# The second half of a two-stage decoder step, rebuilt: one projection stage in fp32r parts and 64 unrolled attention steps

## What is computed

```python
D_MODEL, SEQ, DEC_BATCH, DEC_SEQ, PAST_LEN, PAGE_SIZE = 1024, 1024, 8, 4, 512, 128
H_B, DQK_B, DV_B = 8, 64, 128                  # 8 heads, two maps of 64 each, values of 128

def shared_kv(x, c, g_kv, ada_w_kv, ada_b_kv, w_k, w_v, g_k):
    h, _ = ada_mod(x, c, g_kv, ada_w_kv, ada_b_kv, 2)        # rms_norm, scale, shift
    k = rms_norm((h @ w_k).reshape(b_, t_, H_B, 2, DQK_B), g_k)
    v = (h @ w_v).reshape(b_, t_, H_B, DV_B)
    return k, v                                              # both are outputs too

def diff_weights(s, lam):                                    # s: scores - slope * distance, causal
    p = jax.nn.softmax(s, axis=-1)
    return p[:, :, 0] - lam * p[:, :, 1]

def diff_block(x, c, attend, lam, lam_init, norm_g, ada_w, ada_b, w_in, g_q, g_sub, w_out):
    h, (gate,) = ada_mod(x, c, norm_g, ada_w, ada_b, 3)
    q, z = jnp.split(h @ w_in, [QB], axis=-1)
    q = rms_norm(q.reshape(b_, t_, H_B, 2, DQK_B), g_q)
    o = attend(q, lam)                                       # weights @ v, prompt and sample
    o = rms_norm(o, g_sub) * (1.0 - lam_init)
    out = (o.reshape(b_, t_, ZB) * jax.nn.silu(z)) @ w_out
    return x + gate * out
```

## Time and profile before

| | us |
|---|---|
| median of 3 runs (1944.47 to 1949.61) | 1945.45 |
| the profiled execution | 1949.39 |
| its span, first to last instruction | 1947.7 |
| PE busy | 1770.4 (91%) |
| DVE busy | 717.1 (37%) |
| ACT busy | 712.6 (37%) |
| mean granted clock of PE | 0.915 |

### The profile page before, as it was taken

The page is one execution under the profiler, slowest core; times in us unless marked ns, Lnnn a source line. Parts: engine busy times, 40 slices in busy tenths (PEclk is TensorE's granted clock), DMA queues, the critical chain, the costliest instruction groups (busy, mean ns, idle before and its releaser), DMA issues. The chain is left out here.

```text
span 1947.7 us, 32421 instructions
## 1 busy us (share of the span) xinstructions
PE 1770.4 (91%) x10275; PEld 1406.2 (72%) x10275; DVE 717.1 (37%) x1300; ACT 712.6 (37%) x1261; POOL 234.2 (12%) x373
## 2 busy tenths in 40 slices
PE   6899999999999969698999999989999899998698
PEld 3388889888899759475775666757667577665598
DVE  4527347347446343304123141241321513215321
ACT  2433143143143131434244353353424534344411
POOL 0011001001000000021130210301203012030000
PEclk7999799799799789799899898998989989899799
DMA  8622232232231243332220221112202222021143
GB/s 296 212 66 66 58 120 66 58 120 66 57 120 44 69 146 105 120 91 70 56 87 22 67 72 42 60 58 66 77 24 67 63 67 81 20 69 53 34 121 89
DMA packets 129119, 158.04 MB, mean 81 GB/s; under 512 B 13330, under 2 KB 103985, under 8 KB 129050
## 3 DMA queue, kind: packets, MB, share of 16 engines
q0 software_dynamic: 23776, 73.46, 12.9%
q1 hardware_dynamic: 94330, 70.61, 11.8%
q10 hardware_dynamic: 10944, 12.98, 1.9%
HBM read 127.41 MB, written 29.59 MB: 81 GB/s over the span
## 5 line engine op out<-in xcount | busy, mean ns | idle before, releaser
L1367 PE MATMUL at_psP<-B,w 128*128 128x352 f32 x768 | 251.8, 486 | 16.1 <-ACTq L1514 16.1
L1367 PEld LDWEIGHTS at_psP<-B,w 128*128 128x128 f32 x768 | 153.2, 202 | 102.4 <-issue 31.0
L1352 POOL DMA_DIRECT2D at_vc<-in_cache_v x256 | 139.4, 545 | 275.6 <-issue 275.6
L1091 PE MATMUL op_ps<-op_G_high,op_w_high 128*128 128x352 f32 x384 | 127.0, 331 | 31.2 <-DVE op_G_low L1161 26.2
L581 PE MATMUL gl_psP<-Hh,gl_w_high 128*128 128x352 f32 x384 | 130.2, 339 | 3.6 <-ACT gl_qT L775 2.1
L1376 PE MATMUL at_psP<-w,B 128*128 128x128 f32 (+1 forms) x1152 | 132.4, 275 | 0.0
L1376 PEld LDWEIGHTS at_psP<-w,B 128*128 128x128 f32 (+1 forms) x1152 | 129.6, 183 | 2.7
L581 PE MATMUL gl_psP<-Hl,gl_w_high 128*128 128x352 f32 x384 | 128.5, 335 | 0.0
L581 PE MATMUL gl_psP<-Hh,gl_w_low 128*128 128x352 f32 x384 | 128.2, 334 | 0.0
L1091 PE MATMUL op_ps<-op_G_low,op_w_high 128*128 128x352 f32 x384 | 125.0, 325 | 0.0
L1091 PE MATMUL op_ps<-op_G_high,op_w_low 128*128 128x352 f32 x384 | 124.8, 325 | 0.0
(11 more groups left out here) (257 smaller groups left out, 3284.7 us busy)
## 6 DMA issues: line engine op xcount, KB each, us to landing
at_kc<-in_cache_k SPq DMA_DIRECT2D x256, 64.0 KB, 1.9
at_vc<-in_cache_v POOLq DMA_DIRECT2D x256, 64.0 KB, 2.2
w<-in_w_in_a POOLq DMA_DIRECT2D x24, 512.0 KB, 5.4
gl_wm<-in_ada_w_b POOLq DMA_DIRECT2D x24, 512.0 KB, 5.2
gl_wm<-in_ada_w_kv POOLq DMA_DIRECT2D x16, 512.0 KB, 6.0
su_w<-in_ada_w_a POOLq DMA_DIRECT2D x6, 1024.0 KB, 8.1
su_w<-in_ada_w_a SPq DMA_DIRECT2D x6, 1024.0 KB, 8.7
scr_xT<-B ACTq DMA_DIRECT2D x1, 4224.0 KB, 14.2
```

Source lines behind the costliest of these rows:

```text
L1091: mm = nc.tensor.matmul(ps[:, u % 2, 0:THIRD], ws[:, b, k, :], thirds(gs[:, k, :])[j], start=(k == 0 and n == 0), stop=(k == KC - 1 and n ...
L1352: pool.dma_start(vc[:, bass.ds(n, 1), :], A["cache_v"][bass.ds(page, 1), :, bass.ds(i, 1), :].rearrange("n p h d -> p (n h) d")).then_inc( ...
L1367: mm = nc.tensor.matmul(psP[:, unit % 2, 0:THIRD], w[name][:, k, :], thirds(src[:, k, :])[unit % 3], start=(k == 0), stop=(k == KC - 1))
```

## The change

`setup` and `gla` stay. The first `out_proj` takes its gated input into the residual buffer itself and writes its parts to `Hh` and `Hl`, SP clears used semaphores in it, and `FirstWeights` loads and splits the first projection weights in it (POOL, ACT after tile 3, DVE ahead of tile 6). ACT's table set is named at the start of three blocks.

`project` replaces `normed` and the projections in the heads: 8 blocks of 512 output features (k, k, v, v, q, q, z, z), each over 8 token tiles in two halves h of four, chunks outside, tiles inside, three products of 512 moving columns with the token tile as stationary. Six banks go round. The sample rows are multiplied apart, in fp32, into four column groups of 32 partitions. Squares, sums, roots and scaling follow token-major; normalised q and k are transposed by PE and stored to DRAM scratch, k and v to the outputs; z's gate goes to `B2`. Weight chunks are split one by one as PE frees them.

`attention` reads q, k and v of a head back by DMA, two heads deep, and unrolls 64 steps over all heads: step g has scores(g), values(g - 2) and weigh(g - 1) in PE's list, so that heads run into each other. The first map is no longer normalised: the second is scaled by a ratio and added in one pass, and the row sums enter with the head norm. Page numbers are read once, into 32 registers each on SP and POOL, before any load of SP. Cached keys are transposed in place one head ahead; all 8 sequences' scores are taken in one go in four column groups, and cached values move as 256 columns against 32 stationary weights.

The diff's core:

```diff
-            acc, tmp = sb("no_acc", [P, T], c), sb("no_tmp", [P, 2, KC, SB, SL], c)
-            sq = K["B1"][:, 2:4, :]
-            rs = acc
-            ps = c.enter_context(nc.psum_tensor("no_ps", [P, 4, 512], F32))
-            norm = Norm(nc, K, K["B2"], rs, sq, acc, ps, [(K["B1"], M_B + 8, M_B), (K["B2"], M_KV + 8, M_KV)], 1)
-            out_proj(nc, A["w_out_a"], SCR["xT"], SCR["x1T"], K["B2"], M_A + 16, K, 0, norm, SCR["G"].rearrange("(k p) t -> p k t", p=P))
-            normed(nc, A, K, norm, tmp)
-        attention(nc, A, OUT, K, norm)
...
+            project(nc, A, OUT, SCR, K, norm)
+        attention(nc, A, OUT, SCR, K)
+        out_proj(nc, A["w_out_b"], SCR["x1T"], None, None, M_B + 16, K, 1, OUT=OUT)
...
+                act.preload_act_table_set(NATURAL)
...
+    def load(self, eng):
+        eng.dma_start(self.raw, projection_weights(self.A, 0)).then_inc(self.s_raw, 16)
+    def high(self, eng):
+        eng.wait_ge(self.s_raw, 16)
+        for k in range(KC):
+            self.nc.scalar.activation(self.K["Wh"][:, k, :], self.raw[:, k, :], ACT.Copy).then_inc(self.s_wh, 1)
+    def low(self, eng):
+        mod, vec = self.K["mod"], self.K["vec"]
+        for col, gain in ((M_KV + 8, V_NORM_KV), (M_B + 8, V_NORM_B)):
+            ins = self.nc.vector.scalar_tensor_tensor(mod[:, col:col + 8, :], mod[:, col:col + 8, :], 1.0,
+                                                      bcast(vec[:, gain:gain + 8].unsqueeze(2), P, 8, NC), ALU.add, ALU.mult)
+        ins.then_inc(self.K["sem"]("scales_ready"), 1)
+        for k in range(KC):
+            eng.wait_ge(self.s_wh, k + 1)
+            self.nc.vector.tensor_tensor(self.K["Wl"][:, k, :], self.raw[:, k, :], self.K["Wh"][:, k, :], ALU.subtract).then_inc(self.s_wl, 1)
...
+        BANKS = 6
+        psP = c.enter_context(nc.psum_tensor("pj_psP", [P, BANKS, WB], F32))
...
+                for n, h in halves():
+                    b, half = before(n, h)
+                    for k in range(KC):
+                        if h == 0:
+                            pe.wait_ge(s_wl, KC * n + k + 1)
+                        if n in (0, 4):
+                            pe.wait_ge(s_hl, 16 * (n // 4) + 8 * h + k + 1)
+                        for q in range(4):
+                            t, g = 4 * h + q, 8 * n + 4 * h + q
+                            if k == 0 and g >= BANKS:
+                                pe.wait_ge(s_pev, g - BANKS + 1)
+                            for m, (xs, ws) in enumerate(((Hh, Wh), (Hh, Wl), (Hl, Wh))):
+                                mm = nc.tensor.matmul(psP[:, g % BANKS, :], xs[:, k, t * P:(t + 1) * P], ws[:, k, :],
+                                                      start=(k == 0 and m == 0), stop=(k == KC - 1 and m == 2))
+                            if k == KC - 1:
+                                mm.then_inc(s_pp, 1)
+                            elif h and q == 3:
+                                mm.then_inc(s_wused, 1)
+                        if 1 <= k <= 4 and b >= 0 and normed(b):
+                            turn_tile(8 * b + 4 * half + k - 1)
+                        if h and k == 5 and kind(n) != "v":
+                            turn_samples(n)
+                    if h == 0:
+                        pe.wait_ge(s_raw, 16 * (n + 1))
+                        pe.wait_ge(s_hs, n // 4 + 1)
+                        pe.wait_ge(s_mev, n)
+                        for k in range(KC):
+                            for j in range(4):
+                                mm = nc.tensor.matmul(psM[32 * j:32 * j + 32, 0:P], hs[:, n // 4, k, :], raw[:, k, j * P:(j + 1) * P],
+                                                      start=(k == 0), stop=(k == KC - 1))
...
+                def squares(g):
+                    u = ordinal(g)
+                    act.wait_ge(s_pp, g + 1)
+                    if u >= 2:
+                        act.wait_ge(s_red, u - 1)
+                    A_(sq[:, u % 2, :], psP[:, g % BANKS, :], ACT.Square).then_inc(s_sq, 1)
+                def rstd(g):
+                    u = ordinal(g)
+                    q = g >= 16
+                    act.wait_ge(s_red, u + 1)
+                    A_(rt[:, u % 4, :], ss[:, u % 4, :], ACT.Ln, scale=1.0 if q else 1.0 / DQ, bias=(eps64 if q else eps)[:, 0:1]).then_inc(s_ln, 1)
+                    act.wait_ge(s_ln, u + 1)
+                    A_(rt[:, u % 4, :], rt[:, u % 4, :], ACT.Exp, scale=-0.5).then_inc(s_rt, 1)
...
+                def high(n, k):
+                    if k == 0:
+                        act.wait_ge(s_raw, 16 * (n + 1))
+                    act.wait_ge(*((s_wused, 7 * (n - 1) + k + 1) if k < KC - 1 else (s_pp, 8 * n)))
+                    A_(Wh[:, k, :], raw[:, k, :], ACT.Copy).then_inc(s_wh, 1)
...
+                make(0, 0)
+                make(0, 1)
+                for n, h in halves():
+                    post(n, h)
+                    if h:
+                        sample_post(n)
+                    if (n, h) in ((3, 1), (4, 0)):
+                        make(1, 1 - h)
+                    if h:
+                        for k in range(4):
+                            if n + 1 < NB:
+                                high(n + 1, k)
+                        copy_samples(n)
+                        for k in range(4, KC):
+                            if n + 1 < NB:
+                                high(n + 1, k)
+                post(NB, 0)
...
+                pages = [sp.value_load(pt[0:1, n:n + 1], min_val=0, max_val=A["cache_k"].shape[0] - 1) for n in range(SB * NPG)]
+                for i in range(HB):
+                    if i == 0:
+                        load_qk(0)
+                        load_v(0)
+                    else:
+                        sp.wait_ge(s_ssc, i)
+                    for n in range(SB * NPG):
+                        sp.dma_start(kc[:, n, :], A["cache_k"][bass.ds(pages[n], 1), :, i, :].rearrange("n p d -> p (n d)")).then_inc(s_kc[n // NPG], 16)
+                    if i + 1 < HB:
+                        load_qk(i + 1)
+                        load_v(i + 1)
+                sp.wait_ge(s_ssc, HB)
...
+                def sample_scores(i):
+                    pe.wait_ge(s_cev, use["c", i, SB - 1] + 1)
+                    pe.wait_ge(s_qz, 4 * i + 4)
+                    pe.wait_ge(s_min, 2 * NT * i)
+                    for r in range(2):
+                        for j in range(4):
+                            b = 4 * r + j
+                            nc.tensor.matmul(psS[32 * j:32 * j + 32, 1, :], QZ[:, i % 2, b, :], kc[:, b * NPG:(b + 1) * NPG, :].rearrange("p n d -> p (n d)"),
+                                             start=(r == 0), stop=(r == 1))
+                    for r in range(2):
+                        for j in range(4):
+                            mm = nc.tensor.matmul(psS[32 * j:32 * j + 32, 3, 0:TS], QZ[:, i % 2, 4 * r + j, :], K["ksT"][:, i, :],
+                                                  start=(r == 0), stop=(r == 1))
+                    mm.then_inc(s_ssc, 1)
...
+                def sample_weights(i):
                     pe.wait_ge(s_comb, i + 1)
...
+                def sample_values(i):
                     pe.wait_ge(s_wsT, 2 * (i + 1))
...
+                            both = vc[:, j * NPG + n:(j + 4) * NPG + n + 1:4 * NPG, :]
+                            nc.tensor.matmul(psS[32 * j:32 * j + 32, 3, cols], wsT[:, n, :], both, start=(n == 0), stop=False)
...
+                for b in range(SB):
+                    turn_cache(0, b)
+                for g in range(LAST):
+                    i, t = divmod(g, NT)
+                    if g < STEPS:
+                        scores(g)
+                        if t == 0:
+                            sample_scores(i)
+                        if t == 1:
+                            sample_weights(i)
+                        if t == 2:
+                            sample_values(i)
+                    if 2 <= g < STEPS + 2:
+                        values(g - 2)
+                    if t >= 4 and i + 1 < HB:
+                        turn_cache(i + 1, 2 * (t - 4))
+                    if 1 <= g <= STEPS:
+                        weigh(g - 1, 0)
+                    if t >= 4 and i + 1 < HB:
+                        turn_cache(i + 1, 2 * (t - 4) + 1)
+                    if t == 3 and i < HB:
+                        turn_samples(i)
+                    if t == 0 and i:
+                        turn_out(i - 1, 0)
+                    if t == 4 and i:
+                        turn_out(i - 1, 1)
+                    if 1 <= g <= STEPS and WG(g - 1) == 2:
+                        weigh(g - 1, 1)
...
+                for b in range(0, SB, 2):
+                    copy_cache(0, b)
+                for g in range(LAST):
+                    i, t = divmod(g, NT)
+                    if t >= 4 and i + 1 < HB:
+                        copy_cache(i + 1, 2 * (t - 4))
+                    if 1 <= g <= STEPS:
+                        copy_weights(g - 1)
```

(65 more changed lines are left out.)

1136 lines of the change are left out of this document (708 added, 428 removed).

## The result

The median went from 1947.53 us (four runs, 1944.47 to 1950.49) to 1804.21 (four runs, 1799.69 to 1805.36), a ratio of 0.926 with a 95% interval of 0.9246 to 0.9274. The forecast was 1819 in a range of 1755 to 1885.

What follows compares the result with a forecast made beforehand. PE was taken to bound the second half, with a PE-DVE-ACT ring in the attention steps. Terms 808.5 + 3.4 + 412.5 + 49 + 440.5 + 106.7 gave 1820.6 us; execution overhead and profile offset made it 1819, range 1755 to 1885.

Steps and rivals of the forecast that it cites:

- Projections: Projection stage: 1536 matmuls 0.233 us apart, 358 us; samples 19, turns 17, bank stalls 13, clock at start 3; sum 410.
- Start of attention: Before the first scores: page table, 32 reads, loads and 32 issues stand in a row, 49 us (bounds 26 and 54).
- t = 1: Second step of a head: PE's turn queues behind sample weights waiting for DVE; 8.2 us where 2.8 would do, +5.4.
- t = 2: Third step of a head: sample values hold PE's turn, sample norm and sums precede DVE's combine; 8.2 us, +4.6.
- The clock: Second and third steps of a head: PE falls to 1.2 GHz after idling, 4 us a head, 32 in all.
- the scaling pass: DVE's combine in the 64 steps: dropping the second map's scaling saves 0.56 us a step, 4.5 a head.
- the overlap of two heads: Between heads: the 5.2 us after a head's last combine now overlap the next head.
- Output projection: Last stage: 14.5 us from ACT's first operation to the second third shrink, 6.6 less, to 106.7 with the block's change.
- Table loads: Rival, chance 0.07: loads of 1.28 us stay between Ln and Exp in projection and head roots; +52 us, 1871.
- Exposed loads: Rival, chance 0.04: each of 1536 projection matmuls exposes its stationary load, 0.192 us in full; +295 us, 2114.
- Half clock in all of attention: Rival, chance 0.10: PE stays at its lower clock level through all of attention; +52 us, 1871.
- Cheap ends: Rival, chance 0.13: start of attention takes 26 us and the steps run at full clock; 1764 us.

Runs made afterwards that it cites:

- the last kernel: Changed kernel plus PE's and DVE's reorderings, earlier page reads, and a block's last weight-chunk split behind earlier tiles' squares and scalings: median 1702.93 us, 0.944 of the changed kernel's.

## Why the prediction was right, and where its terms were off

The direction, the size and the order of the parts held: 22.6 us of 1820.6 separate the sum from the span. Five steps of the table came out shorter, by 30.0 us together, and three longer, by 7.4, so the sum is not right by cancelling; within the 64 steps there is some luck, as said below. The 3 us taken off because the profiled execution of before lay above its median had the wrong sign here, where it lay below.

**Projections: right, by its parts.** Matmuls 0.231 apart against 0.233, 355 of 358 us. From the starts on PE, the samples cost 16 (19), the turns 15 (17), the bank stalls 13 (13), the clock at the start and after the stalls 5 (3). Four stalls of 2.1 beyond the usual step and three of 0.8 stand where the prediction put them; the mechanism (squares behind the split) is shown by the last kernel. One row was read too freely: the 256 columns of the earlier trace rows had stationary tiles of 32 columns, which load less, so the row did not show that a load of 128 hides at 256. The same trace has the rows that do: 748 steps of L581 with 256 columns behind a load of 128, 0.113 apart at the median. In the projections it is 0.120, by the narrower matmuls.

**Start of attention: right mechanism, size 7 too long.** The reads were priced well (0.57 for 0.6), and moving them took 19.0 us off. The page table took 1.2 us to the first read and not 2.9. The issue took 0.52 and not 0.7, a price that rested on splitting 1.6 us of a loop by an estimate; from the first issue to the first scores it is 21.2 us and not 25.0, and the turns through one bank, which the sum has as one last turn only, end no earlier than the issues.

**The steps: right for t = 1, too long at t = 2.** I had 8.2 and 2 for the clock at t = 1; it is 10.2. At t = 2 I had the same 10.2; it is 7.85. The clock is the wrong term. It falls behind both waits, as forecast, but the second low stretch comes too late for t = 2: at t = 2 the clock was back at 1.00 (1428.30 to 1438.30), and filling the wait at t = 1 left t = 2 as it was. The first stretch costs 2.3 us a head, 16 in seven. The second lies in t = 3 and t = 4, for which the sum has no clock at all. In the two heads in which it starts in t = 3 and reaches furthest into t = 4, t = 4 takes 7.01 us, and in the three in which it ends in t = 3, 5.11, the same as with DVE's order changed; the mean is 5.99. By this estimate the second stretch costs 0.9 a head, 6 in seven, so 22 us for the clock and not 32. The Trainium skill (TensorE: Matmul & The Clock Gate, section Why this matters for your kernels) states that pauses between bursts bring the half clock back; this trace agrees for the wait of 3.88 us, behind which the clock was 0.50 and 16 products took 3.78. The other six steps come to 34.0 us against the 33.9 that remain in the prediction, and that is luck in part: the scaling pass is worth 2.4 us a head and not 4.5, and the overlap of two heads more than the 5.2 that it was booked at (9.9, measured with both lists reordered). These two misses have opposite signs and do not cancel; what makes up the rest is not shown.

**Output projection: wrong, a misread row.** I took the row at 1849.45 in the earlier trace rows for the second third of the first tile. It is the third one. The first and the second, in the timeline of PE before:

```profile
1837.90 0.63 PE L1091 MATMUL op_ps<-op_G_high,op_w_high 128*128 128x352 f32 x1 [9.81 <-DVE op_G_low L1161]
...
1843.30 0.32 PE L1091 MATMUL op_ps<-op_G_high,op_w_high 128*128 128x352 f32 x1
```

From ACT's first operation to the third third it was 14.45 us and is now 13.54 (1699.70 less 1686.16), so the gain was 0.9 and not 6.6. The weight tile takes the 2.4 that I had, but a table load of 1.28 now stands ahead of it, and the first third takes 6.04 us where it took 5.40. So the second third starts 9.7 us after ACT's first operation, where it was 8.3 before and 7.9 in the sum. What the work on G gives back by leaving DVE's list is PE's wait of 2.17 us ahead of the third third.

**The rivals.** Table loads: shown by undoing the one line; they would have cost some 70 us and not 52, as the projections have 48 of it where 20 were counted. Exposed loads: the margin at 512 columns is 0.231 against 0.111. Half clock in all of attention: 0.87 in the heads, so no. Cheap ends: no, the start of attention took 42.4 us and not 26, and the steps lost some 22 us to the clock.

## What to carry to other kernels

In a pipeline over several engines, look for the step that is too long for its size, and see what stands in each list between a result and its user: moving a few lines in three lists (PE's, DVE's, ACT's) gave 62 us of the 64 steps, with no work taken away. A side job (samples, a weight split) belongs behind the main chain's next link in every list that it shares with it, and scalar reads of addresses belong in a stage where the issuing engine is idle. A wait on PE of some 4 us was paid twice here, the second time in the clock of what followed.
